# The forget rows' sum and exp moved one step down on VectorE and ScalarE in the attention phase

## The reference

```python
def mixer_attention(x, w_in, b_f, w_out, rel_bias):
    h = x @ w_in                              # columns: q,k,v of MoBA, q,k,v of FoX, 8 forget logits
    ...
    f_logit = (h[..., 3 * wa + 3 * wb:] + b_f).astype(jnp.float32)
    log_f = jax.nn.log_sigmoid(f_logit).transpose(0, 2, 1)
    o_a = moba_attention(qkv_a[0], qkv_a[1], qkv_a[2], rel_bias)
    o_b = forgetting_attention(qkv_b[0], qkv_b[1], qkv_b[2], log_f)
    ...
# forgetting_attention: c = cumsum(log_f); softmax(q k^T / sqrt(d) + c_t - c_s) v, causal
```

## Time and profile before

| | before |
|---|---|
| median of 3 runs | 1002.44 us (1002.22 to 1002.56) |
| the profiled execution's own time | 1002.16 us |
| its span, first to last instruction | 1000.4 us |
| TensorE busy | 992.9 us, 99% of the span |
| VectorE busy | 705.2 us, 70% |
| ScalarE busy | 458.3 us, 46% |
| GpSimd busy | 44.7 us, 4% |
| mean granted TensorE clock | 1.000 of full speed |

### The profile page before, as it was taken

The page is one execution under the profiler, slowest core; times in us unless marked ns, Lnnn a source line. Parts: engine busy times, 40 slices in busy tenths (PEclk is TensorE's granted clock), DMA queues, the critical chain, the costliest instruction groups (busy, mean ns, idle before and its releaser), DMA issues.

```text
span 1000.4 us, 13938 instructions
## 1 busy us (share of the span) xinstructions
PE 992.9 (99%) x5372; PEld 849.6 (85%) x5372; DVE 705.2 (70%) x875; ACT 458.3 (46%) x523; POOL 44.7 (4%) x57
## 2 busy tenths in 40 slices
PE   9999999999999999999999999999999999999998
PEld 7888888879877888888888888888898888888887
DVE  5866666778678766666786766667787876666684
ACT  5444344246564553434355443434354553434441
POOL 0500000100001000000010000000210000000010
PEclk9999999999999999999999999999999999999999
DMA  8965656456236676565547756565467676565631
GB/s 286 286 228 170 211 171 214 131 177 201 85 127 204 217 233 213 170 213 171 175 162 254 239 173 213 169 215 175 150 191 236 212 236 214 169 213 169 215 128 43
DMA packets 129831, 191.51 MB, mean 191 GB/s; under 512 B 5464, under 2 KB 95832, under 8 KB 129792
## 3 DMA queue, kind: packets, MB, share of 16 engines
q1 hardware_dynamic: 126432, 180.11, 54.6%
q0 software_dynamic: 3072, 10.61, 3.0%
q10 hardware_dynamic: 288, 0.26, 0.1%
HBM read 189.90 MB, written 1.06 MB: 191 GB/s over the span
## 4 chain that ended last, share of the span: by engine, by line
PE 94%; DVE 3%; DMA 1%; ACT 1%; issue 0%; SPq 0%; DVEq 0%; ACTq 0%
PE gu L599 26%; PE gu L607 14%; PE acc L417 9%; PE acc L418 9%; PE acc L419 9%; PE gu L417 5%; PE gu L419 5%; PE gu L418 5%; PE tp L512 2%; PE gu L813 2%; PE gu L901 2%; DVE g_lo L1294 1%; PE gu L794 1%; PE gu L818 1%; PE gu L906 1%; DMA rawA<-in_ffn_w_up 1%
## 5 line engine op out<-in xcount | busy, mean ns | idle before, releaser
L599 PE MATMUL gu<-xT,g_hi 128*128 128x512 f32 x1152 | 274.6, 390 | 0.0
L599 PEld LDWEIGHTS gu<-xT,g_hi 128*128 128x128 f32 x1152 | 215.6, 188 | 44.4
L607 PEld LDWEIGHTS gu<-xT,g_lo 128*128 128x128 f32 x1152 | 147.7, 191 | 5.6
L1442 DVE TENSOR_REDUCE stage<-gu 128x256 f32<-128x512 f32 x72 | 49.7, 690 | 145.6 <-PE gu L607 145.6
L1294 DVE TENSOR_TENSOR g_lo<-rawA,g_hi 128x2048 fp32r<-128x2048 f32 (+2 forms) x65 | 139.6, 2150 | 17.6 <-ACT g_hi L967 17.5
L607 PE MATMUL gu<-xT,g_lo 128*128 128x256 f32 x1152 | 149.4, 283 | 0.0
L1294 DVE TENSOR_TENSOR g_lo<-rawB,g_hi 128x2048 fp32r<-128x2048 f32 (+1 forms) x64 | 138.6, 2166 | 10.6 <-ACT g_hi L967 10.5
L417 PE MATMUL acc<-d_hi,hT_hi 128*128 128x512 f32 x352 | 138.6, 394 | 0.0
L418 PE MATMUL acc<-d_lo,hT_hi 128*128 128x512 f32 x352 | 137.9, 392 | 0.0
L967 ACT ACTIVATE g_hi<-rawA 128x2048 fp32r<-128x2048 f32 (+2 forms) x66 | 118.0, 1793 | 41.9 <-DMA rawA<-in_ffn_w_up 16.3
L419 PE MATMUL acc<-d_hi,hT_lo 128*128 128x512 f32 x352 | 137.0, 389 | 0.0
(11 more groups left out here) (205 smaller groups left out, 1007.4 us busy)
## 6 DMA issues: line engine op xcount, KB each, us to landing
rawD<-in_ffn_w_down SPq DMA_DIRECT2D x44, 1024.0 KB, 5.5
rawA<-in_ffn_w_gate SPq DMA_DIRECT2D x42, 512.0 KB, 4.0
rawA<-in_ffn_w_up SPq DMA_DIRECT2D x42, 512.0 KB, 5.0
rawB<-in_ffn_w_gate SPq DMA_DIRECT2D x42, 512.0 KB, 3.9
rawB<-in_ffn_w_up SPq DMA_DIRECT2D x42, 512.0 KB, 4.9
rawA<-in_attn_w_in SPq DMA_DIRECT2D x12, 512.0 KB, 4.4
rawB<-in_attn_w_in SPq DMA_DIRECT2D x12, 512.0 KB, 4.8
rawA<-in_ple_w_gate SPq DMA_DIRECT2D x8, 512.0 KB, 4.8
```

The lines of the kernel that those rows point to most:

```text
L599: pe.matmul(bank[:, :], g_hi[:, slot, b, at:at + P], xT[:, b, :, :].rearrange("p i t -> p (i t)"), start=b == 0, stop=False)
L607: done = pe.matmul(bank[:, 0:S], g_lo[:, slot, b, at:at + P], xT[:, b, 0, :], start=False, stop=b == KB - 1)
L1442: dve.tensor_reduce(gates, gu[0][:, :].rearrange("p (i t) -> p t i", i=2), AXX, ALU.add).then_inc(gate_sum, 1)
```

## The change

Two moves, and nothing added or taken away. On VectorE the forget sum goes from its own entry in the list (ahead of `("g", 1, 0)`) into the wide half (1, 0), behind the low part of block 2's first half and ahead of the two bank sums. The `("exp",)` entry goes behind `("g", 1, 1)`: on ScalarE the exp follows the high part of block 2's second half, and on VectorE the exp chain follows all of the steps of the wide half (1, 1). TensorE still does its forget matmuls where it did.

```diff
-WIDE_STEPS = {(1, 0): ("low", 0, 1), (1, 1): (0, 1, "low"), (2, 0): (0, 1, "low"), (2, 1): (0, "low", 1)}
+WIDE_STEPS = {(1, 0): ("low", "forget", 0, 1), (1, 1): (0, 1, "low"), (2, 0): (0, 1, "low"), (2, 1): (0, "low", 1)}
 ATTN_ORDER = [
     ("g", 0, 0), ("g", 0, 1), ("forget",),
-    ("g", 1, 0), ("exp",), ("g", 1, 1), 
+    ("g", 1, 0), ("g", 1, 1), ("exp",),
     ("g", 2, 0), ("pT", 0), ("g", 2, 1), ("log",),
...
+                    def forget_sum():
+
+                        dve.wait_ge(rows_loaded, 32)
+                        dve.wait_ge(f_mm, 1)
+                        dve.tensor_reduce(lf[:, 6, :], acc[0][0:HEADS, 0, :].rearrange("p (i t) -> p t i", i=2),
+                                          AXX, ALU.add).then_inc(step, 1)
+                        dve.tensor_copy(lf[:, 7, :], acc[0][LO_ROW:LO_ROW + HEADS, 0, 0:S]).then_inc(step, 1)
+                        steps[0] += 2
+                        dve.wait_ge(step, steps[0])
+                        link(dve.scalar_tensor_tensor(out=lf[:, 6, :], in0=lf[:, 6, :], scalar=bf_col,
+                                                      in1=lf[:, 7, :], op0=ALU.add, op1=ALU.add))
+                        link(dve.tensor_scalar(lf[:, 7, :], lf[:, 6, :], -1.0, None, ALU.mult))
+                        dve.tensor_tensor(lf[:, 2, :], lf[:, 6, :], lf[:, 7, :], ALU.min).then_inc(f_arg, 1)
...
                                     if part == "low":
                                         lo_g(g0 + c + 1, h)
+                                    elif part == "forget":
+                                        forget_sum()
                                     else:
                                         qk_sum(c, h, part)
```

More of the change, by code:

```diff
@@ L1585, in _ @@
                                 pT_hi[:, h, :, :]).then_inc(tp_taken[h], 1)
[L1586 to L1597, removed]
                         elif e[0] == "exp":
```

## The result

The changed kernel takes 1007.92 us (median of 5 runs, 1007.6 to 1008.12) against 1002.44 us before (now of 5 runs, 1002.22 to 1002.85): 5.5 us more, a ratio of 1.0055 (1.0045 to 1.0066). Slower was forecast, by 3.9 us. The span of the profiled execution grew from 1000.4 to 1006.2 us, and TensorE's busy time from 992.9 to 995.3 us. In all ratios of this document two far slower executions are left out: one of 1089.3 us at a granted clock of 0.851, among the 12 of the kernel with the forget sum between the two bank sums, and one of 2410.2 us of the kernel before.

The account below looks back on a forecast made before the run. TensorE, busy for 99% of the span, was taken as the bound. Two waits, 2.4 + 1.5 = 3.9 us, on the 1002.44 us median gave 1006.3 us; the range for 8 in 10 was 1004.7 to 1008.0 us.

Parts of the forecast that it names:

- main case: Both waits of TensorE come, +3.0 to +4.1 us, 1005.4 to 1006.6 us; 78 in 100.
- rival B: Clock falls to 1.2 GHz in (1, 1) after the longer wait; 0 to 5.8 us on top, 1009 us named; 13 in 100.
- signs of being wrong: Low part at 210.77 starting earlier, forget sum under 2.39 us, no wait before (2, 1), granted clock leaving 1.00.
- First wait, +2.4: TensorE before half (1, 1): the forget sum delays the bank sum; +2.4 us, wait grows from 0.93 to 3.3 us.
- Second wait, +1.5: TensorE before half (2, 1): the exp chain delays the bank sums of (2, 0); +1.5 us, a new wait.
- The rest passes it on: TensorE from 232 us to the end: listed waits total 0.9 us, so at most that much can be absorbed.
- rival C: Not slower: weight loads such as that at 299.27 us absorb the delay; 1002.4 us with all absorbed; 4 in 100.
- Rival A: Only the wait before (1, 1) costs, none before (2, 1); +2.4 us, 1004.8 us; 5 in 100.
- The exp chain's old place was free, the copy of ScalarE is worth nothing: Matmuls of (1, 1) covered the chain, so removing it gains nothing; the `rawB` copy's earlier start, up to 1.6 us, gains nothing.
- Busy times of all engines stay as they are: Expected in the changed kernel's profile: no engine's busy time changes, while the span grows to about 1004.3 us.

## Why the prediction was right or wrong

The direction held, and so did the two waits with their places and releasers; the forecast of 1006.3 us was 1.6 us too low. The measured 1007.92 us lies outside the main case (1005.4 to 1006.6), and inside the range for 8 in 10 (to 1008.0) by 0.08 us, only because that range took in a part of rival B. That it held so narrowly is luck. The sum lacked a term that came true, and one of the prediction's own signs of being wrong came: the granted clock left 1.00 behind the first wait.

- *First wait, +2.4.* Right: 2.47 in the trace, 3.40 us of wait where 3.2 to 3.4 was named. The forget sum alone, moved, shows it. The low part didn't start quite when it did: 0.44 us later (211.21), of which 0.27 is the offset of this execution and 0.17 came with the load.
- *Second wait, +1.5.* Right: 1.50 in the trace, with an idle time of 1.28 us; the exp entry alone, moved, gives +1.65 us.
- *The rest passes it on.* Right, and the allowance of up to 0.9 us for what might be absorbed wasn't needed: the lag is 5.79 us at block 3 and 5.8 us at the end. With that, rival C falls. Rival A falls with the second wait.
- *The exp chain's old place was free, the copy of ScalarE is worth nothing.* Right. The copy from `rawB` started at 212.49 us against 212.37 before, as its load had only just landed; of the "up to 1.6 us sooner" nothing came.
- *The clock.* This is the step that failed. The sum of 3.9 us put the clock at nothing, and rival B was given 13 in 100, on the ground that matmuls are dense on both sides of the wait. Density around the wait did not help: the clock fell in both profiled kernels with a wait of 3.4 us, and in all 10 of their runs the mean granted clock is 0.998. Rival B had the place right. Its price, named as 0 to 5.8 us with 1009 us (2.7) as the value, was 1.6 us: of the half's 32 matmuls only those between 218.1 and 221.5 us ran at 1.2 GHz. The reading behind it was weak too: the row of 40 slices looks the same with the fall in it. "Busy times of all engines stay as they are" failed with the clock: TensorE's grew by 2.4 us. The rule that the Trainium skill ("TensorE: Matmul & The Clock Gate", section "Why this matters for your kernels") gives, that an idle gap can put the clock back to half rate, is borne out here (3.40 us of idle time, then a granted clock of 0.50 from 219 to 221 us), and it spoke against this change. I should have let it carry more than the absence of such a gap from the trace of before.

## What to carry to other kernels

On an engine that serves a saturated TensorE, the place of a small instruction is worth more than its length: 2.39 us cost nothing where VectorE waited for a load anyway, 1.4 us between two bank sums, and 3.8 us in front of both. Before moving work off an idle stretch, ask what stands next in that engine's order and who waits for it. When TensorE's wait grows from one microsecond to several, put the clock on the bill as a term of its own (1.6 to 2.1 us here; in a part of the executions already behind waits of 1.7 to 2.8 us), and look for it in the mean granted clock and in narrow windows, not in the row of 40 slices. And small work that doesn't fit a gap as a whole may fit as pieces.

## What the runs showed of the hardware that I hadn't expected

The clock can fall after the wait is over, and not always at the same point: with waits of 3.40 and 3.38 us it fell 1.5 us after the matmuls had begun in one execution (218.1 us), and 0.6 us after in the other (217.6 us). How long it stays down doesn't follow the wait closely. It was 3.4 us in all three profiled executions with waits of 2.76, 3.38 and 3.40 us (to 220.3, 221.0 and 221.5 us), at a price of 1.6 us each, and 6.8 us (216.8 to 223.6) behind a wait of 5.34 us, at a price of 2.1 us, since 2.2 us of it fell into the wait. Useless matmuls in the wait bring the time back, by 1.6 us over the stretch. And one kernel can have more than one time: with 2.8 us of idle time, three runs at 1004.5 to 1004.8 us with a mean granted clock of 1.000, and five at 1005.9 to 1006.6 us with 0.998. What decides between the two in one execution, the runs don't show.
